# Merged activations kept in SBUF, and dt weight parts stacked, in a hybrid decoder kernel

## Chip, cores and metric

One Trainium2 chip, one of its cores. The metric is the device time of one execution in microseconds, as the median of several.

## What is computed

One layer of a decoder that serves 1024 prompt tokens and 8 x 4 sample tokens, 1056 together, all in fp32. The parts that matter here:

```python
proj = xn @ w_in                      # z | xBC | dt (24 columns) | u | v
dt = softplus(dt_raw + dt_bias)       # 24 heads
a_out = y @ w_a_proj                  # y: (tokens, 1536), after the state space scan
b_out = spatial_gating(u, v) @ w_b_proj
gates = sigmoid(xn @ w_gate + b_gate)
merged = gates[:, :1024] * a_out + gates[:, 1024:] * b_out
x = x + merged @ w_out
x = x + cross_attend(rmsnorm(x), mem_k, mem_v, w_mem_q, w_mem_o)
x = x + hier_moe(x)
```

## The kernel before

Every product is made in three passes (`matmul3`, L277): operands are split into a high part (fp32r) and a low remainder, and high x high, high x low and low x high are accumulated in one PSUM bank. ScalarE makes the high part (a copy), VectorE the low part (a subtraction). The kernel is a row of blocks (stages); the instructions of each engine are written out by hand and tied by semaphores, and all engines meet at a block's end. P is 128, T is 1056, a slab is T / 3 = 352 tokens, BANK is 512 columns, NC = 8 prompt tiles of 128 tokens, NT = 9 with the sample tile, DK = 8 blocks of 128 features.

**stage_rows** (L352) makes v and z by token tiles. After the first round of its nine tiles it makes the dt projection (L541 to L546): for each of three slabs and eight k, one `matmul3` with the 24 weight columns as the stationary operand, so 72 matmuls with 352 moving columns. VectorE copies the result from PSUM to dtT (L744). PE makes the first tile of the next round and then transposes dtT (L531 to L535), and the softplus follows. VectorE makes the low parts of the next weight (L704) ahead of that copy.

**stage_sample_merge** (L1566) ends with eight products, one for each block f of 128 features of merged: 12 k x 3 slabs x 3 passes with the y activations of 1056 columns moving (L1937, a loop on PE). For each f ScalarE and VectorE split the weight (L2017, L2177), VectorE multiplies the gates with the product (`gated`, L2193), GpSimd adds the two gated halves (L1800) into `m_out`, and ScalarE issues the store of that tile to `merged_scr` in HBM (L2056). The last f is gated, added and stored by slabs (L2062, L2208). SyncE loads the gates of the next f once the addition has read them (L1746, L1766). SyncE has loaded the first half of w_out to SBUF in this stage too (`query_w`, L1761). At the end SyncE waits for the stores and reloads the first token tile (L1776), and PE runs eight warming matmuls (`keep_busy`, L1965), each of which is two instructions in the trace.

**stage_out_query** (L2215) starts with `keep_busy` of twelve. Its product is by token tiles: `product(j, c)` for column half j of w_out and tile c, 8 k x 3 passes with 512 columns moving, so 24 matmuls (L2340); `sample_product` is the plain fp32 product of the 32 sample tokens (L2331). The order on PE is product(0,0), sample(0), product(0,1..7), sample(1), product(1,0..7), with the transposes of the normed tiles (`turn`, L2357) from product(1,2) on. Four PSUM banks go round (MB), so a product waits for the addition of the one four places earlier. SyncE (L2272) reloads merged from HBM (sample columns, then three pieces), loads x in one transfer of 4 MB and the sample rows in another, then the second half of w_out in four pieces (each wants its piece of the first half split and two products done), the gain row of the next norm (L2297) and the first four tiles of the query weight (`load_q`). ScalarE (L2403) splits the w_out pieces and the tiles (`w_high`, `high`), VectorE makes the low parts (`w_low`, `low`), and only then adds products to x (`add`, L2493), waiting for all of x (L2519). For the second half it makes w_low(1, 0..3), add(0,7), two query low parts (`q_low`), waits for the gain (L2532), adds the sample product, and then for each tile c: add(1,c), h_low(c-2), normed(c). ScalarE squares each added tile, and GpSimd makes its root mean square (L2318). `turn(c)` waits for normed(c) and h_low(c-1).

## Time and profile before

| | us |
|---|---|
| Median of 3 executions (lowest, highest) | 2085.32 (2078.94, 2086.09) |
| Profiled execution: its time | 2082.61 |
| Its span, first to last instruction | 2080.9 |
| Mean granted TensorE clock, share of full | 0.981 |

The profile is of one execution. Times in it count from the span's start. PE is TensorE's matmuls, PEld its weight loads, DVE VectorE, ACT ScalarE, POOL GpSimd, SP SyncE; an engine's name with a q is its instruction sequencer, which issues DMAs. A matmul's listed duration is longer than the distance to the next, since they are pipelined: for the cost of one, take the distance between starts. "Idle before" is the time in which the engine had nothing running ahead of the instruction, with who released it.

### The profile page before, as it was taken

The page shows a single profiled execution, that of the slowest core. Times are in us where ns is not written, and L with a number is a line of the kernel's source. Part 1 is how long each engine was busy: PE and PEld are TensorE (multiplying, and loading weights), DVE is VectorE, ACT ScalarE, POOL GpSimd, SP SyncE. Part 2 cuts the span into 40 slices and gives each one's busy share as a digit, 9 for nine tenths or more (in the row PEclk, how much of TensorE's full clock was granted, in tenths as well). Part 3 has the DMA queues.
Part 4 walks back from the last instruction along what each step waited for, and adds up shares of the span by engine and source line. Part 5 has one row for each costly group of instructions (what it writes and reads, how often), then busy time and mean ns, then how long its engine had stood idle before and what let it go on. Part 6 is the DMA issues. An engine that isn't in the chain of part 4 may idle for free. (4 is left out here: it accounts for less than half of the span.)

```text
span 2080.9 us, 32851 instructions
## 1 busy us (share of the span) xinstructions
PE 1968.3 (95%) x12220; PEld 1747.1 (84%) x12221; DVE 1033.5 (50%) x1201; ACT 749.7 (36%) x1089; POOL 394.9 (19%) x510
## 2 busy tenths in 40 slices
PE   7999999999999999898999999999999899998995
PEld 5788899999888888788998789888788788877884
DVE  4215254552565656466113341335633675886775
ACT  4322122222334444443002121423412264774674
POOL 2000100000343444431111000000000122223225
PEclk9999999999999999989999999999999899999998
DMA  5122233333334334398546211344404568998987
GB/s 198 58 88 68 67 92 101 82 83 91 97 116 122 111 113 125 103 311 281 180 139 216 84 61 41 107 167 163 154 36 165 205 218 274 331 372 289 318 303 275
DMA packets 247476, 333.02 MB, mean 160 GB/s; under 512 B 16269, under 2 KB 163629, under 8 KB 247329
## 3 DMA queue, kind: packets, MB, share of 16 engines
q1 hardware_dynamic: 211268, 276.25, 39.5%
q0 software_dynamic: 7344, 25.38, 4.7%
q10 hardware_dynamic: 28768, 30.02, 4.1%
q8 instruction: 71, 1.16, 0.2%
q14 instruction: 25, 0.20, 0.0%
HBM read 255.30 MB, written 77.61 MB: 160 GB/s over the span
## 5 line engine op out<-in xcount | busy, mean ns | idle before, releaser
L3932 ACT ACTIVATE e_w_high<-big 128x2048 fp32r<-128x2048 f32 x94 | 176.4, 1911 | 46.4 <-PEq L3018 20.7
L279 PE MATMUL psum<-hT_high,t_w_high 128*128 128x352 f32 x576 | 186.9, 324 | 0.3 <-DVE t_w_low L1022 0.3
L281 PE MATMUL psum<-hT_high,t_w_low 128*128 128x352 f32 x576 | 185.6, 322 | 0.0
L280 PE MATMUL psum<-hT_low,t_w_high 128*128 128x352 f32 x576 | 185.6, 322 | 0.0
L4073 DVE TENSOR_TENSOR e_w_low<-big,e_w_high 128x2048 fp32r<-128x2048 f32 x64 | 144.0, 2288 | 33.1 <-ACT e_w_high L3932 26.2
L279 PE MATMUL psum<-hT_high,s_w_high 128*128 128x352 f32 x384 | 131.8, 343 | 0.0
L280 PE MATMUL psum<-hT_low,s_w_high 128*128 128x352 f32 x384 | 125.1, 326 | 0.0
L281 PE MATMUL psum<-hT_high,s_w_low 128*128 128x352 f32 x384 | 124.8, 325 | 0.0
L3811 PE MATMUL psum<-e_w_high,e_xT 128*128 128x512 f32 x272 | 107.4, 395 | 3.7 <-DVE e_xT L4069 3.0
L279 PEld LDWEIGHTS psum<-hT_high,t_w_high 128*128 128x128 f32 x576 | 108.1, 188 | 0.5 <-DVE t_w_low L1022 0.4
L280 PEld LDWEIGHTS psum<-hT_low,t_w_high 128*128 128x128 f32 x576 | 108.2, 188 | 0.0
L281 PEld LDWEIGHTS psum<-hT_high,t_w_low 128*128 128x128 f32 x576 | 108.1, 188 | 0.0
L3813 PE MATMUL psum<-e_w_high,e_xT 128*128 128x512 f32 x272 | 106.1, 390 | 0.0
L3812 PE MATMUL psum<-e_w_low,e_xT 128*128 128x512 f32 x272 | 106.0, 390 | 0.0
L279 PE MATMUL psum<-r_w_high,hT_high 128*128 128x512 f32 x256 | 101.6, 397 | 4.6 <-DVE hT_low L700 4.6
L280 PE MATMUL psum<-r_w_low,hT_high 128*128 128x512 f32 x256 | 100.5, 392 | 0.0
L281 PE MATMUL psum<-r_w_high,hT_low 128*128 128x512 f32 x256 | 100.4, 392 | 0.0
L4111 DVE TENSOR_TENSOR e_w_low<-big,e_w_high 128x2048 fp32r<-128x2048 f32 x30 | 68.1, 2290 | 52.1 <-ACT e_w_high L3932 52.0
L1040 DVE SCALAR_TENSOR_TENSOR t_conv_out<-t_conv_in,veca,t_conv_out 128x1080 f32<-128x1080 f32 x60 | 80.7, 1344 | 7.5 <-DVE t_conv_out L1040 1.2
L279 PE MATMUL psum<-yT_high,m_w_high 128*128 128x352 f32 x252 | 81.6, 324 | 0.0
L280 PE MATMUL psum<-yT_low,m_w_high 128*128 128x352 f32 x252 | 81.4, 323 | 0.0
L281 PE MATMUL psum<-yT_high,m_w_low 128*128 128x352 f32 x252 | 81.0, 321 | 0.0
(590 smaller groups left out, 4907.0 us busy)
## 6 DMA issues: line engine op xcount, KB each, us to landing
big<-in_w_expert_gate SPq DMA_DIRECT2D x32, 1024.0 KB, 8.3
big<-in_w_expert_up SPq DMA_DIRECT2D x32, 1024.0 KB, 11.0
big<-in_w_expert_down SPq DMA_DIRECT2D x32, 1024.0 KB, 13.3
t_w<-in_w_in SPq DMA_DIRECT2D x24, 512.0 KB, 4.6
m_gates<-gate_scr SPq DMA_DIRECT2D x22, 528.0 KB, 5.7
x_scr<-t_conv_out ACTq DMA_DIRECT2D x20, 512.0 KB, 4.3
gate_scr<-s_gate_tanh ACTq DMA_DIRECT2D x16, 528.0 KB, 3.4
scan_w<-in_w_gate SPq DMA_DIRECT2D x16, 512.0 KB, 4.1
```

What stands on the lines that cost most here:

```text
L279: nc.tensor.matmul(out, ah, w_h, start=start, stop=False)
L280: nc.tensor.matmul(out, ah, w_l, start=False, stop=False)
L281: return nc.tensor.matmul(out, al, w_h, start=False, stop=stop)
L1040: op = nc.vector.scalar_tensor_tensor(o, c[:, j:j + CB_OUT], wk[j], o, ALU.mult, ALU.add)
L3811: nc.tensor.matmul(ps[:, bank, :], ah[:, k, :], w_h, start=(k == 0), stop=False)
L3812: nc.tensor.matmul(ps[:, bank, :], ah[:, k, :], w_l, start=False, stop=False)
L3813: mm = nc.tensor.matmul(ps[:, bank, :], al[:, k, :], w_h, start=False, stop=(k == kt - 1))
L3932: return nc.scalar.activation(dst, src, ACT.Copy)
L4073: nc.vector.tensor_tensor(wl[:, p, :], raw[:, p, :], wh[:, p, :].bitcast(F32), ALU.subtract).then_inc(s_wl, 1)
L4111: nc.vector.tensor_tensor(wl[:, p, :], raw[:, p, :], wh[:, p, :].bitcast(F32), ALU.subtract).then_inc(s_dl, 1)
```

## The change

Three edits.

In stage_rows the high and low parts of the dt weight stand side by side in one tile of 64 columns (24 + 8 zeros, twice). Each k takes two matmuls (high and low activations) instead of three, and the result has the high-weight sums in partitions 0 to 23 and the low-weight sums in 32 to 55. VectorE copies the second to dtT and adds the first. t1 shares its place with wdt.

In stage_sample_merge GpSimd writes each merged tile to its own place in SBUF (five behind `big`, three further up), and nothing is stored to or reloaded from HBM. ScalarE and VectorE split the first 128 tokens of each tile, and after the first half of the last merge product ScalarE makes the four high parts of the first half of w_out; VectorE makes three low parts. PE, in place of the eight warming matmuls, runs k = 0 to 5 of product(0, 0) into PSUM bank 0; k = 6 and 7 follow behind the block's end and the twelve warming matmuls. The loops over f are written out on ScalarE, VectorE and GpSimd.

In stage_out_query x comes in nine transfers, one for each tile with a semaphore of its own, tiles 0, sample, 1 to 5 at once and 6 and 7 once product(0,0) is done. The high and low parts of a token tile are made by two operations each (five tiles of features and three). The gain row, the first query weights, their high parts and the last low piece of the second half of w_out use places of the merged tiles, so they wait for sample(1) (s_mm of order(1, NC) + 1) and for the last low part. The order on the queues: SyncE's gain load goes from before sample(1) to behind it, and `load_q` behind that; ScalarE's `high(0)` stands last of the eight.

```diff
+    HS = 32
...
+        wdt_or_t1 = g.sb("r_wdt_then_t1", [P, NT * H], ctx=ctx)
+        wdt = wdt_or_t1[:, 0:DK * H].rearrange("p (k h) -> p k h", h=H)
+        t1 = wdt_or_t1.rearrange("p (c h) -> p c h", h=H)
+        wdts = g.sb("r_wdt_parts", [P, DK, 2, HS], F32R, ctx=ctx)
+        wdth, wdtl = wdts[:, :, 0, 0:H], wdts[:, :, 1, 0:H]
...
-                            mm = matmul3(nc, ps[0:H, 3 + n, 0:SLAB], wdth[:, k, :], wdtl[:, k, :],
-                                         hh[:, k, xs_], hl[:, k, xs_], k == 0, k == DK - 1)
+                            parts = wdts[:, k].rearrange("p a h -> p (a h)")
+                            nc.tensor.matmul(ps[0:2 * HS, 3 + n, 0:SLAB], parts, hh[:, k, xs_], start=(k == 0), stop=False)
+                            mm = nc.tensor.matmul(ps[0:2 * HS, 3 + n, 0:SLAB], parts, hl[:, k, xs_], start=False,
+                                                  stop=(k == DK - 1))
...
+            nc.vector.memset(wdts[:].bitcast(F32)[:, :, :, H:HS], 0.0)
...
-            nc.vector.tensor_copy(dtT[:, 0:T].rearrange("p (n t) -> p n t", t=SLAB),
-                                  ps[0:H, 3:6, 0:SLAB]).then_inc(s_dte, 1)
+            dt_slabs = dtT[:, 0:T].rearrange("p (n t) -> p n t", t=SLAB)
+            nc.vector.tensor_copy(dt_slabs, ps[HS:HS + H, 3:6, 0:SLAB]).then_inc(s_dtl, 1)
+            dve.wait_ge(s_dtl, 1)
+            nc.vector.tensor_tensor(dt_slabs, dt_slabs, ps[0:H, 3:6, 0:SLAB], ALU.add).then_inc(s_dte, 1)
...
+class OutFirst:
+
+
+    EARLY = 3
     def __init__(self, g):
         alloc = g.nc.alloc_semaphore
-        self.s_stored = [alloc(f"last_merged_stored{n}") for n in range(3)]
-        self.s_first = alloc("first_act_loaded")
-        self.at = g.R1T
-        self.src = g.merged_scr
-
-    def load_first(self, sp):
-
-        sp.wait_ge(self.s_stored[0], 16)
-        sp.dma_start(self.at[:, :, 0:P], self.src[:, :, 0:P].rearrange("k p t -> p k t")).then_inc(self.s_first, 16)
-
-
-def stage_sample_merge(g, top, query_w, act_in):
+        at = g.big_at
+        mix_at = at + 2 * NT * D * 4
+        lower, upper = g.alias32("merged_lower", [P, 5, T], mix_at), g.alias32("merged_upper", [P, 3, T], MERGED_AT)
+        self.parts = ((slice(0, 5), lower), (slice(5, DK), upper))
+        self.tiles = [lower[:, f] for f in range(5)] + [upper[:, f] for f in range(3)]
+        self.ah = g.alias("first_act_high", [P, DK, P], at + (NT + 6) * D * 4)
+        self.al = g.alias("first_act_low", [P, DK, P], at + (NT + 7) * D * 4)
+        piece = [P, 2, BANK]
+        self.wh = [g.alias(f"v_w_high{p}", piece, OUT_PARTS_AT + p * 8192) for p in range(3)]
+        self.wl = [g.alias(f"v_w_low{p}", piece, OUT_PARTS_AT + p * 8192 + 4096) for p in range(3)]
+        self.wh.append(g.alias("v_w_high3", piece, OUT_PARTS_AT - 4096))
+        self.wl.append(g.alias("v_w_low3", piece, OUT_LAST_AT))
+        self.wl_second = self.wl[0:3] + [g.alias("v_w_low3_second", piece, mix_at + 4096)]
+        self.s_wh, self.s_wl, self.s_ah, self.s_al = (alloc("first_out_" + n) for n in (
+            "w_high", "w_low", "act_high", "act_low"))
...
-            sp.wait_ge(s_mst[0], 16 * (DK // 2))
-            sp.wait_ge(s_mst[1], 16 * (DK // 2 - 1))
-
-            sp.wait_ge(s_lm, 3)
-            act_in.load_first(sp)
...
+            for f in range(DK - 1):
+                pool.wait_ge(s_pr, f + 2)
+                nc.gpsimd.tensor_tensor(out.tiles[f], gt[:, 0, :], gt[:, 1, :], ALU.add).then_inc(s_ad, 1)
...
+                nc.gpsimd.tensor_tensor(out.tiles[DK - 1][:, x], gt[:, 0, x], gt[:, 1, x], ALU.add).then_inc(s_la, 1)
...
-            g.keep_busy(6, 8)
+            pe.wait_ge(s_pr, DK)
+            for k in range(2 * out.EARLY):
+                if k % 2 == 0:
+                    pe.wait_ge(out.s_wl, k // 2 + 1)
+                pe.wait_ge(out.s_al, k + 1)
+                matmul3(nc, ps[:, 0, :], out.ah[:, k, :], out.al[:, k, :], out.wh[k // 2][:, k % 2, :],
+                        out.wl[k // 2][:, k % 2, :], k == 0, False)
...
+            def first_high(f):
+                nc.scalar.activation(out.ah[:, f, :], out.tiles[f][:, 0:P], ACT.Copy).then_inc(out.s_ah, 1)
+
+            for f in range(DK - 1):
+                for k in range(2):
+                    if f:
+                        act.wait_ge(s_mh, f * 2 + k + 1)
+                    w_high(f + 1, k, wh)
                 act.wait_ge(s_ad, f + 1)
-                act.dma_start(g.merged_scr[f], mo[:, s, :]).then_inc(s_mst[s], 16)
-
-            tile(0, 0, True, False)
-            with act.Fori(0, DK // 2 - 1) as i:
-                for s in range(2):
-                    tile(i * 2 + 1 + s, 1 - s, True, True)
-            for n in range(3):
-                x = slice(n * SLAB, (n + 1) * SLAB)
-                act.wait_ge(s_la, n + 1)
-                act.dma_start(g.merged_scr[DK - 1][:, x], mo[:, 1, x]).then_inc(act_in.s_stored[n], 16)
+                first_high(f)
+            act.wait_ge(s_qw, 64)
+            act.wait_ge(s_mh, 2 * DK - 1)
+            for p in range(out.EARLY + 1):
+                nc.scalar.activation(out.wh[p][:], query_raw[:, 2 * p:2 * p + 2, :], ACT.Copy).then_inc(out.s_wh, 1)
+            act.wait_ge(s_la, 1)
+            first_high(DK - 1)
...
+            def first_low(f):
+                dve.wait_ge(out.s_ah, f + 1)
+                tt(out.al[:, f, :], out.tiles[f][:, 0:P], out.ah[:, f, :].bitcast(F32), ALU.subtract).then_inc(out.s_al, 1)
+
+            def out_w_low(p):
+                dve.wait_ge(out.s_wh, p + 1)
+                tt(out.wl[p][:], query_raw[:, 2 * p:2 * p + 2, :], out.wh[p][:].bitcast(F32), ALU.subtract).then_inc(out.s_wl, 1)
+
+            for f in range(DK - 1):
+                following(f)
+                gated(f, 3 * (f % 2))
+                if f:
+                    first_low(f - 1)
+            first_low(DK - 2)
+            out_w_low(0)
+            out_w_low(1)
             dve.wait_ge(s_gt, DK * 32)
             for n in range(3):
+                if n == 1:
+                    out_w_low(2)
                 x = slice(n * SLAB, (n + 1) * SLAB)
                 dve.wait_ge(s_lm, n + 1)
                 stt(gt[:, 0, x], gt[:, 0, x], 1.0, ps[:, 3 + n, 0:SLAB], ALU.add, ALU.mult).then_inc(s_lg, 1)
-
-
-def stage_out_query(g, x, x_dram, w, qT, qT_at, kv_at, mem, act_in):
+            first_low(DK - 1)
...
+            def load_x(t):
+                src = d["x_prompt"][0][t * P:(t + 1) * P, :] if t < NC else d["x_sample"].rearrange("b t n -> (b t) n")
+                sp.dma_start(x[0:rows(t), t, :], src).then_inc(s_x[t], 16)
+
+            load_x(0)
+            sp.wait_ge(s_z, 1)
+            load_x(NC)
+            for t in range(1, 6):
+                load_x(t)
+            sp.wait_ge(s_mm, 1)
+            for t in range(6, NC):
+                load_x(t)
             for p in range(PW):
                 sp.wait_ge(s_wl, p + 1)
                 sp.wait_ge(s_mm, 2)
                 load_w(1, p)
+            sp.wait_ge(s_mm, order(1, NC) + 1)
+            sp.wait_ge(s_al, NC)
...
+                first = j == 0 and c == 0
+                if j == 0 and c:
+
+                    pe.wait_ge(s_al, c)
+                if j and c == 0:
+                    pe.wait_ge(s_al, NC)
                 if n >= MB:
                     pe.wait_ge(s_ad, n - MB + 1)
-                for k in range(DK):
+                for k in range(2 * out.EARLY if first else 0, DK):
                     if c == 0 and k % 2 == 0:
                         pe.wait_ge(s_wl, PW * j + k // 2 + 1)
-                    mm = matmul3(nc, ps[:, n % MB, :], ah[:, k, cols(c)], al[:, k, cols(c)], wh[:, k, :],
-                                 wl[:, k, :], k == 0, k == DK - 1)
+                    a_h, a_l = (out.ah[:, k, :], out.al[:, k, :]) if first else (ah[:, k, cols(c)], al[:, k, cols(c)])
+                    mm = matmul3(nc, ps[:, n % MB, :], a_h, a_l, wh[k // 2][:, k % 2, :],
+                                 wls[j][k // 2][:, k % 2, :], k == 0, k == DK - 1)
...
+            act.sem_inc(s_wh, PW)
...
+                for k, part in out.parts:
+                    op = nc.scalar.activation(ah[:, k, cols(c)], part[:, :, cols(c)], ACT.Copy)
+                op.then_inc(s_ah, 1)
...
-            w_high(0, 0)
-            high(0)
-            for p in range(1, PW):
-                w_high(0, p)
             for c in range(1, NC):
                 high(c)
+            high(0)
             for p in range(PW):
                 w_high(1, p)
+            act.wait_ge(s_mm, order(1, NC) + 1)
+            act.wait_ge(s_al, NC)
             for q in range(2):
                 q_high(0, q)
...
+            dve.sem_inc(s_wl, out.EARLY)
...
+                dve.wait_ge(s_ah, c if c else NC)
+                for k, part in out.parts:
+                    op = nc.vector.tensor_tensor(al[:, k, cols(c)], part[:, :, cols(c)], ah[:, k, cols(c)].bitcast(F32),
+                                                 ALU.subtract)
+                op.then_inc(s_al, 1)
...
+                    dve.wait_ge(s_x[c], 16)
...
+            w_low(0, PW - 1)
             for c in range(1, NC):
                 low(c)
-            dve.wait_ge(s_x, 16 * len(x_dram))
+            low(0)
             add(0, 0)
             add_sample(0, order(0, NC))
             for c in range(1, NC - 1):
                 add(0, c)
-            for p in range(PW):
+            for p in range(PW - 1):
                 w_low(1, p)
             add(0, NC - 1)
+            dve.wait_ge(s_mm, order(1, NC) + 1)
+            w_low(1, PW - 1)
             dve.wait_ge(s_wl, 2 * PW)
-            dve.wait_ge(s_mm, order(1, NC) + 1)
             for q in range(2):
                 q_low(q, q)
             dve.wait_ge(s_gr, 16)
```

## Rows read from the trace of the kernel before

**Rows 1.** The page, part 1: busy time of each engine.

```profile
...
PE 1968.3 (95%) x12220; PEld 1747.1 (84%) x12221; DVE 1033.5 (50%) x1201; ACT 749.7 (36%) x1089; POOL 394.9 (19%) x510
```

**Rows 2.** Waits, 1100 to 1240 us: who waited, for whom, total, times, longest.

```profile
...
DVE big L2497 <- DMA big<-in_x_sample: 8.7, 1, 8.7
...
PE psum L279 <- DVE big L2497: 4.6, 1, 4.6
...
PE psum L128 <- PEq L133: 2.0, 1, 2.0
PE psum L2362 <- DVE R_low L2506: 1.8, 2, 0.9
```

**Rows 3.** Groups by line, 60 to 95 us: count, busy and mean ns, idle before.

```profile
...
L279 PEld LDWEIGHTS psum<-hT_high,r_wdt_high 128*24 128x24 f32 x24 | 2.4, 101 | 1.5 <-issue 0.2
...
L744 DVE COPY r_dtT<-psum 24x1056 f32<-24x1056 f32 x1 | 1.2, 1245 | 11.1 <-PE psum L281 11.1
```

**Rows 4.** Timeline of PE, dt projection: start, length, operation.

```profile
...
73.55 0.34 PE L279 MATMUL psum<-hT_high,r_wdt_high 128*24 128x352 f32 x1
...
85.04 0.39 PE L279 MATMUL psum<-r_w_high,hT_high 128*128 128x512 f32 x1
...
90.59 0.73 PE L533 MATMUL psum<-ident,r_dtT 24*128 24x24 f32 x9
```

**Rows 5.** Groups by line, 1070 to 1112 us, in the merge.

```profile
...
L279 PEld LDWEIGHTS psum<-yT_high,m_w_high 128*128 128x128 f32 x87 | 16.3, 188 | 0.0
...
L2179 DVE SCALAR_TENSOR_TENSOR m_w_low<-m_w,m_w_high 128x768 fp32r<-128x768 f32 x4 | 3.8, 958 | 28.4 <-ACT m_w_high L2019 28.4
```

**Rows 6.** Timeline of PE, from the last merge product to the second half.

```profile
...
1115.08 1.95 PE L128 MATMUL psum<-ident 128*128 128x128 f32 x16
1119.07 4.54 PE L128 MATMUL psum<-ident 128*128 128x128 f32 x24 [2.05 <-PEq L133]
1123.37 0.48 PE L279 MATMUL psum<-v_w_high,v_act_high 128*128 128x512 f32 x1
...
1129.02 1.95 PE L2336 MATMUL psum<-v_w,big 128*32 128x128 f32 x64
...
1141.69 0.39 PE L281 MATMUL psum<-v_w_high,R_low 128*128 128x512 f32 x1
1146.68 0.47 PE L279 MATMUL psum<-v_w_high,v_act_high 128*128 128x512 f32 x1 [4.61 <-DVE big L2497]
...
1175.70 1.95 PE L2336 MATMUL psum<-v_w,big 128*32 128x128 f32 x64
1177.58 0.50 PE L279 MATMUL psum<-v_w_high,v_act_high 128*128 128x512 f32 x1
```

**Rows 7.** Busy time by window: length, each engine's busy (count), PEclk, DMA share.

```profile
...
1147.00:1151.00 4.00, 4.00 (x12) 3.14 (x11) 1.87 (x5) 0.00 (x0) 0.00 (x0) 0.57 1.05 380
```

**Rows 8.** Timeline of ACT, end of the merge stage.

```profile
...
1112.03 5.14 ACTq L2065 DMA_DIRECT2D merged_scr<-m_out  x3
```

**Rows 9.** Timeline of DVE after the second sample product.

```profile
...
1178.70 2.35 DVE L2511 TENSOR_TENSOR v_q_w_low<-v_q_w,v_q_w_high 128x1024 fp32r<-128x1024 f32 x2
...
1183.35 0.69 DVE L2497 TENSOR_TENSOR big<-big,psum 128x512 f32<-128x512 f32 x1 [1.22 <-PE psum L281]
...
1188.79 0.69 DVE L2497 TENSOR_TENSOR big<-big,psum 128x512 f32<-128x512 f32 x1 [1.33 <-PE psum L281]
...
1197.27 1.23 DVE L2506 TENSOR_TENSOR R_low<-psum,v_act_high 128x1024 fp32r<-128x1024 f32 x1 [2.34 <-ACT v_act_high L2434]
```

**Rows 10.** Timeline of PE, the second transpose of the output stage.

```profile
...
1200.37 1.03 PE L2362 MATMUL psum<-ident,v_xn 128*128 128x128 f32 x8
```

**Rows 11.** DMA issues, whole run: destination, queue, KB each, us to landing.

```profile
...
big<-in_x_prompt SPq DMA_DIRECT2D x1, 4096.0 KB, 20.5
...
gain_row<-in_norm_mix SPq DMA_DIRECT2D x1, 512.0 KB, 5.2
```

**Rows 12.** The same, 1178 to 1240 us.

```profile
...
v_q_w<-in_w_mem_q SPq DMA_DIRECT2D x2, 512.0 KB, 4.5
```

More of the change, by code:

```diff
@@ L138 @@
 OUT_W_AT = 212960
+MERGED_AT = 197952
+OUT_PARTS_AT = 120032
+OUT_LAST_AT = 181472
 SUMS_AT = 221696
@@ L429, in _ @@
             with nc.allow_non_contiguous_dma(reason="24 columns of dt"):
[L430 removed]
+                sp.dma_start(wdt, w_in[:, :, COL_DT:COL_DT + H]).then_inc(s_wdt, 16)
             sp.dma_start(w[:, 1], w_in[:, :, first_col[1]:first_col[1] + BANK]).then_inc(s_w[1], 16)
@@ L633, in _ @@
             act.wait_ge(s_wdt, 16)
-            nc.scalar.activation(wdth[:], wdt[:], ACT.Copy).then_inc(s_dh, 1)
+            nc.scalar.activation(wdth, wdt, ACT.Copy).then_inc(s_dh, 1)
             act.wait_ge(first.s_alog, 16)
@@ L721, in _ @@
             dve.wait_ge(s_dh, 1)
-            nc.vector.tensor_tensor(wdtl[:], wdt[:], wdth[:].bitcast(F32), ALU.subtract).then_inc(s_dl, 1)
+            nc.vector.tensor_tensor(wdtl, wdt, wdth.bitcast(F32), ALU.subtract).then_inc(s_dl, 1)
             for c in range(2, NT):
@@ L753, in _ @@
             ch.done(nc.vector.tensor_scalar(g.dt[:], t2[:], 0.0, None, ALU.max))
-            ch.done(nc.vector.tensor_tensor(g.dt[:], g.dt[:], t1[:], ALU.add))
+            ch.done(nc.vector.tensor_tensor(g.dt[:], g.dt[:], t1, ALU.add))
             ch.done(nc.vector.tensor_tensor(g.dta[:], g.dt[:], mid(g.aneg[:], NT), ALU.mult))
@@ L763, in _ @@
             dve.wait_ge(s_act, 4)
-            ch.done(nc.vector.tensor_tensor(g.dte[:], g.dt[:], t1[:], ALU.mult))
+            ch.done(nc.vector.tensor_tensor(g.dte[:], g.dt[:], t1, ALU.mult))
             w_low(3)
@@ L1657, in stage_sample_merge @@
         s_mh, s_pr, s_ad = g.sem("m_half_product"), g.sem("m_gated"), g.sem("m_added")
-        s_mst = [g.sem(f"m_stored{i}") for i in range(2)]
         s_lm, s_lg, s_la = (g.sem("m_last_" + x) for x in ("product", "gated", "added"))
@@ L2046, in _ @@
             act.wait_ge(s_bm, CHUNKS)
-            def tile(f, s, more, waits):
-                if more:
-                    for k in range(2):
-                        if waits:
-                            act.wait_ge(s_mh, f * 2 + k + 1)
-                        w_high(f + 1, k, wh)
-                act.wait_ge(s_ad, f + 1)
-                act.dma_start(g.merged_scr[f], mo[:, s, :]).then_inc(s_mst[s], 16)
-            tile(0, 0, True, False)
-            with act.Fori(0, DK // 2 - 1) as i:
-                for s in range(2):
-                    tile(i * 2 + 1 + s, 1 - s, True, True)
-            for n in range(3):
-                x = slice(n * SLAB, (n + 1) * SLAB)
-                act.wait_ge(s_la, n + 1)
-                act.dma_start(g.merged_scr[DK - 1][:, x], mo[:, 1, x]).then_inc(act_in.s_stored[n], 16)
+            def first_high(f):
[5 more added lines that the diff above has]
+                    w_high(f + 1, k, wh)
+                act.wait_ge(s_ad, f + 1)
+                first_high(f)
[5 more added lines that the diff above has]
+            first_high(DK - 1)
         @block.vector
@@ L2238, in stage_out_query @@
         s_w = [[g.sem(f"v_w_loaded{j}_{p}") for p in range(PW)] for j in range(2)]
-        s_x, s_gr = g.sem("v_x_loaded"), g.sem("v_gain_loaded")
-        s_a = [g.sem(f"v_act_loaded{i}") for i in range(AP_)]
-        s_as = g.sem("v_sample_act_loaded")
+        s_x, s_gr = [g.sem(f"v_x_loaded{t}") for t in range(NT)], g.sem("v_gain_loaded")
         s_uw = [g.sem(f"v_q_w_loaded{i}") for i in range(2)]
-        s_z, s_az, s_mm, s_ad, s_ah, s_al, s_wh, s_wl, s_wf = (g.sem("v_" + n) for n in (
-            "x_padded", "act_padded", "product", "added", "act_high", "act_low", "w_high", "w_low", "w_parts_used"))
+        s_z, s_mm, s_ad, s_ah, s_al, s_wh, s_wl, s_wf = (g.sem("v_" + n) for n in (
+            "x_padded", "product", "added", "act_high", "act_low", "w_high", "w_low", "w_parts_used"))
         s_sq, s_ms, s_rs, s_xn, s_tr, s_hh, s_hl = (g.sem("v_" + n) for n in (
@@ L2316, in _ @@
             nc.gpsimd.memset(x[:, NT - 1, :], 0.0).then_inc(s_z, 1)
-            nc.gpsimd.memset(act_T[:, :, T:TP], 0.0).then_inc(s_az, 1)
             for c in range(NT):
@@ L2511, in q_low @@
                 nc.vector.tensor_tensor(ul[:, q], uw[:, q], uh[:, q].bitcast(F32), ALU.subtract).then_inc(s_ul, 1)
-            w_low(0, 0)
-            low(0)
-            for p in range(1, PW):
-                w_low(0, p)
+            w_low(0, PW - 1)
             for c in range(1, NC):
                 low(c)
-            dve.wait_ge(s_x, 16 * len(x_dram))
+            low(0)
             add(0, 0)
```

92 lines of the change are left out of this document (20 added, 72 removed).

## The prediction

> **What bounds the kernel now.** I first read the busy shares of the page: PE works 95% of the span, no other engine over half [rows 1]. So a change pays where it takes matmuls off PE, or removes a hole in PE's stream. Next I read the waits of the stretch that the diff touches [rows 2]. PE has three holes there: 2.0 us at the stage boundary, 4.6 us waiting for an addition on VectorE, and 1.8 us in two late transposes. VectorE itself sat 8.7 us behind the load of x, so the second hole is x arriving late. The timeline puts it between the third and the fourth output product [rows 6]. After it the granted clock is 0.57 of full for four microseconds, so for most of them the lower level, 1.2 GHz [rows 7]. Last, the dt projection: 72 matmuls without a hole from 73.55 to 85.04 us, 0.1596 us each [rows 4].
>
> **The dt projection.** It goes from 72 matmuls to 48: high and low columns of the weight stand together as 64 weight columns, and each is multiplied by high and low activations. 24 x 0.1596 = 3.83 us less on PE. What no row shows is a weight load of 64 columns. One of 24 takes 101 ns [rows 3] and one of 128 takes 188 [rows 5]; but beside the 128-column loads, too, 264 matmuls of 352 columns pass in 42 us (three groups like that of the row), 0.159 each. So the load is hidden at both sizes and I take 0. Were it not hidden, interpolation gives 34 ns more for each of 48, 1.6 us back. The Trainium skill (TensorE: Matmul & The Clock Gate, "Back-to-back issue gap" and "LDWEIGHTS") says that the spacing is set by both operations and that a load takes columns / 1.2 ns; by that, as an estimate, 53 ns against 20, and the saving would be 2.2 us instead of 3.8. The equal spacings at 24 and at 128 columns speak against it.
>
> The parts must now be added on VectorE: after the copy of 1.25 us comes an addition of about the same length. It is hidden. VectorE had waited 11.1 us for this product [rows 3], and PE wants dtT only behind one more product, 5.55 us later [rows 4]; 2 x 1.25 plus a semaphore leaves 2.8 us. The memset of the padding columns and the strided writes of the parts fall into VectorE's and ScalarE's idle time at the start; t1 taking wdt's place moves nothing.
>
> **Across the stage boundary.** The eight warming matmuls (16 instructions, 1.95 us) go [rows 6]. In their place come 18 matmuls of the first output product (k 0 to 5), about 0.23 us each, so 4.1 us of work that was behind the boundary: moved, not saved. The last arrival there was PE at 1117.03 and ScalarE, issuing stores, at 1117.17 [rows 6, 8]. Now PE arrives alone at 1115.08 + 18 x 0.23 + 0.16 of drain = 1119.4, and I keep the 2.04 us of boundary and the twelve warmers with their 4.3 us behind it. Saved: 1.95 - 0.16 = 1.79. An accumulation left open in PSUM over a boundary stands in no row; it waits for nothing, so 0, and at worst one more boundary, 2.0.
>
> Its cover: the operands must be ready by 1115. The output weight's four high parts start when the first half of the last merge product is through, 54 x 0.16 = 8.6 before 1115.08, so at 1106.4; four ScalarE copies of about 1.05 end at 1110.7. VectorE makes two low parts (1.2 each, from 128x768 at 0.96 [rows 5]) before the last gates, the third after the first gate slab; it is there by about 1114 and wanted 12 matmuls after 1115. The 128x128 splits of each merged tile (two per tile, each under 0.3) and the unrolled loops of the three engines lie in merge products of 108 x 0.16 = 17.3 us. The merged stores and reloads (4.3 MB each way) vanish and no one on the path waits for their absence except as follows.
>
> **x per tile.** x used to queue behind the merged reload, landing 20.5 us after its issue [rows 11]. Now x tile 0 is the first transfer of the new stage. At about 400 GB/s a 512 KB tile is 1.3 us; five tiles and the sample are there some 9 us after the boundary, the last two, which wait for the first product, by 12. VectorE adds tile 0 only after its nine splits. These are now pairs of operations because the merged tiles lie in two places. A pair is between 1.2 (one of 128x1024) and 1.9 (two of 0.96 [rows 5]); I take 1.4, near the sum of elements plus one start. 1.2 + 8 x 1.4 = 12.4, the first addition ends at 13.1 after the boundary; the fourth product wants it at 4.3 + 1.5 + 2.0 + 10.9 = 18.7. With 1.9 it is 17.1, still in time. So the hole goes: from 1141.92 to 1146.68, 4.76 us, and with it 4.0 x (1 - 0.57) = 1.72 us of slow clock [rows 6, 7]. Next late is nothing until the second half.
>
> **What is moved back.** The gain row and the first two query weights used to be issued around 1140 us. Now they alias the merged tiles and wait for the second sample product (call its end T, 1177.58 before [rows 6]). ScalarE's and VectorE's query splits wait with them, and VectorE's additions stand queued behind. The price: a gain broadcast landed 5.2 us after its issue [rows 11]; two more 512 KB transfers behind it at 1.3 each: the second query weight lands at T + 0.1 + 5.2 + 2.6 = T + 7.9. The bounds are 4.7, a query pair alone [rows 12], with nothing for the gain, and 20.5, the worst load there is [rows 11]. After landing, its high and low part end 2.26 later, T + 10.2; before, that was 1181.05, T + 3.5 [rows 9]: 6.7 late. Slack: VectorE's idle 1.22, 1.33 and again 1.33 before three additions [rows 9], then 1.87 between the first low part done at 1198.50 and the transpose that wants it at 1200.37 [rows 9, 10]. Together 5.8, so PE loses 0.9 us: the landing less 7.0. From then on VectorE catches up 1 us per tile.
>
> **The sum** against the profiled execution (2082.61 us, span 2080.9): -3.83 - 1.79 - 4.76 - 1.72 + 0.9 = -11.2, giving 2071.4. The median shown is 2.7 above that execution, so 2085.3 - 11.2 = 2074.1. A measurement of this kernel can tell about 0.5%, 10.4 us, from no change; the forecast is barely over it.
>
> **Rivals.**
> (a) The moved loads bite harder. If they land as crowded as the old stage's loads, say 13 us after issue, the loss is 13.4 - 7.0 = 6.4 plus 1.7 of clock behind the new hole: 12.1 - 8.1 = 4.0 left, 2081. For: these loads are now on a wait chain. Against: nothing else uses the queue at that moment, and a pair took 4.5 [rows 12]. Chance 0.12.
> (b) The same place, on the other side: a landing of 20.5 [rows 11] costs 13.5 + 1.7 = 15.2 against 12.1, so +3.1, 2088.4. It decides from a landing of 17.4. That needs eight times the megabytes in the queue. Chance 0.03.
> (c) The x hole only changes its name: additions late behind VectorE's splits or a tile of x. Then the 6.5 us stay, 2080.6. It needs 5.6 us of extra delay. Chance 0.07.
> (d) Part of the change does not do what it says: the 64-column weight loads show (1.6 back) or the boundary takes longer (up to 2.0). 2076 to 2078. Chance 0.12.
> The forecast itself: 0.66.
>
> **How the numbers follow.** The best case has no loss at T and reads 2073.2 against the median; the three executions shown spread over 7 us, which I allow as 3.5 either way, and the median stood near their upper end, so low 2067.5. Upwards (d) and most of (a) and (c) are taken in: 2080.5. Faster by over 0.5% needs under 2074.9: of the forecast's 0.66 about 0.48, of (d) 0.03, and 0.03 for a low draw of the rest, 0.54. Slower by over 0.5% needs +10.4, far over (b)'s price, so it takes an unforeseen cause: 0.04. The rest, 0.42, is within.
>
> **What would show it.** 48 matmuls of 352 columns in the dt projection at 0.16 apart, dtT read without a hole; 18 matmuls between the last merge product and the boundary and no warmers; the output stage's first half from boundary to second sample product 48 us instead of 58.5, with no VectorE wait on x and a clock of 1.00; the second query weight landing near T + 8 and about 1 us of new PE wait before the second or third transpose. Wrong would be a weight-load-bound dt spacing, a hole over 2 us after T, or PE waiting at 1115 for the output weight's low parts.

## The result and the profile after

The changed kernel takes 2066.16 us (median; 2063.97 to 2067.87 over 4 runs), the kernel before 2082.94 beside it (2078.94 to 2086.09): ratio 0.9917, interval 0.9904 to 0.9929, so 16.8 us less by the medians where 11.2 were forecast, and 1.3 under the forecast's lower end of 2067.5. The profiled executions differ by 16.7 (2082.61 and 2065.92; spans 2080.9 and 2064.0). The forecast of 2074.1 also stood on a median of three, 2085.3, which is 2.4 above the later one; the other 5.6 us are gain that it did not see.

TensorE's busy time fell from that of [rows 1] by 14.3 us; the other engines do slightly more. The page of the changed kernel, part 1:

```profile
PE 1954.0 (95%) x12180; PEld 1737.1 (84%) x12181; DVE 1036.8 (50%) x1219; ACT 753.2 (36%) x1105; POOL 399.3 (19%) x509
```

**The dt projection**, groups by line (60 to 95 us), then the timeline of PE, against [rows 3, 4]:

```profile
L550 PE MATMUL psum<-hT_high,r_wdt_parts 128*64 128x352 f32 x24 | 7.7, 324 | 0.0
...
L551 PEld LDWEIGHTS psum<-hT_low,r_wdt_parts 128*64 128x64 f32 x24 | 3.2, 135 | 0.6
```

```profile
73.78 0.37 PE L550 MATMUL psum<-hT_high,r_wdt_parts 128*64 128x352 f32 x1
...
81.52 0.39 PE L282 MATMUL psum<-r_w_high,hT_high 128*128 128x512 f32 x1
```

48 matmuls in 7.74 us are 0.161 each: the 64-column loads take 135 ns, between the 101 and 188 that bounded them, and do not show in the spacing.

**From the merge to the output stage**, timeline of PE, against [rows 6]:

```profile
1108.81 0.39 PE L282 MATMUL psum<-v_w_high,first_act_high 128*128 128x512 f32 x1
...
1112.69 0.39 PE L284 MATMUL psum<-v_w_high,first_act_low 128*128 128x512 f32 x1
1114.80 2.92 PE L128 MATMUL psum<-ident 128*128 128x128 f32 x24 [1.73 <-PEq L133]
1117.47 0.48 PE L282 MATMUL psum<-v_w_high,first_act_high 128*128 128x512 f32 x1
```

The 18 moved matmuls run without a gap. But the boundary's idle time is 1.73 us, not 2.05, and the same 24 warming instructions take 2.92 us, not 4.54: the granted clock over them and their wait is 1.00 of full, where it was 0.60 in the kernel before, the lower of its two levels for most of the time. From the first of them to the end of the second sample product it is 46.3 us, where the prediction wrote 48. There is no hole for x; from here on PE has no wait longer than a microsecond to the second sample product, which ends at 1161.12. **Behind it** ScalarE, then PE's transpose:

```profile
1167.53 1.06 ACT L2448 ACTIVATE v_q_w_high<-v_q_w 128x1024 fp32r<-128x1024 f32 x1 [7.07 <-DMA v_q_w<-in_w_mem_q]
1169.12 1.06 ACT L2448 ACTIVATE v_q_w_high<-v_q_w 128x1024 fp32r<-128x1024 f32 x1 [0.53 <-DMA v_q_w<-in_w_mem_q]
```

```profile
1184.77 1.06 PE L2374 MATMUL psum<-ident,v_xn 128*128 128x128 f32 x8 [0.70 <-DVE R_low L2522]
```

The second query weight is there 8.0 us behind the end of the sample product (forecast 7.9), and PE loses 0.9.

Read by PE's milestones (the starts of the first matmuls of each part), the change of each stretch, in us, in two pairs of profiles (the second pair, taken later, is e11 and e12):

| stretch | forecast | first pair | second pair |
|---|---|---|---|
| start of the run to the dt projection | 0 | +0.2 | +1.4 |
| dt projection | -3.8 | -3.75 | -3.75 |
| from there to the first product of the next stage | 0 | -0.9 | -0.8 |
| to the first merge product | 0 | -1.9 | -1.0 |
| merge, boundary, first half of the output stage | -8.3 | -10.2 | -10.0 |
| second half, to the first query product | +0.9 | +0.9 | +1.0 |
| all that follows | 0 | -0.8 | -1.6 |
| to the last matmul | -11.2 | -16.4 | -14.7 |

So the forecast terms came as forecast, and three things came on top: 1.9 us at the boundary, 0.8 to 0.9 behind the rows stage, and 2.6 to 2.7 spread over other stages, against which 0.2 and 1.4 were lost ahead of the dt projection.

### The profile page after: what moved, and what is told of

It is laid out like the page before. It is cut to its first block and busy times, and to the rows that moved or that the text cites. A ratio compares the mean times of both kernels' runs of the same rounds, so it can differ in the third digit from the quotient of the medians.

```text
span 2064.0 us, 32742 instructions
## 1 busy us (share of the span) xinstructions
PE 1954.0 (95%) x12180; PEld 1737.1 (84%) x12181; DVE 1036.8 (50%) x1219; ACT 753.2 (36%) x1105; POOL 399.3 (19%) x509
```

## The experiments

All times of the kernel before beside them lie at 2082.3 to 2083.6 (medians of 7 to 19 executions), but for e16's single 2084.2. A gain is taken from the ratio. Where there is one execution (e9, e10, e11, e13, e14, e16), its time means little and the trace decides.

**The parts alone.** e1 is the kernel before with only the dt edit; e2 is the changed kernel with the dt edit undone.

> The kernel before with the dt edit alone. Both theories: the dt projection 3.8 us shorter on PE (24 matmuls of 352 columns at 0.16), nothing of it given back. Theory A (chance: the part of the gain beyond the sum of terms is granted clock that happened to fall at stage boundaries in the profiled execution of before and not in that of after): -3.5 to -3.8 us in time, and the profile shows slow stretches at some of the boundaries near 521, 1115 and 1491 us, in no fixed pattern. Theory B (the boundaries behave by what runs around them): the 3.5 us earlier arrival changes nothing at the boundaries, slow stretches near 1115 as in the profile of before.

> The changed kernel with the dt projection as it was. By the terms of the prediction without dt: 1.8 (warmers) + 4.8 (wait for x) + 1.7 (clock behind it) - 0.7 (the moved loads, as the profile of after shows it) = -7.6 us. Theory A: -7.6 on average, with a spread of 2 us by the clock. Theory B (the first output products ahead of the boundary keep the clock up over it): -9.6 to -10, and the twelve warmers take 2.7 us in the profile, not 4.3.

e1: 2078.18, ratio 0.9979 (0.997 to 0.9988), 4.4 us less; its milestones are at -3.4 behind the dt projection, -4.3 at the next stage's start. e2: 2072.83, ratio 0.9954 (0.994 to 0.9967), 9.6 less. In e2's profile the stretch from the merge to the second sample product is shorter by 10.2 us, as in the changed kernel; that profile is of the fastest of its five executions (2066.99), 5.8 below their median. The sum of the two is 14.0 with an uncertainty of 3.4; nothing shows that the parts work on each other. The dt edit makes 0.9 us at a place that it doesn't touch (below).

**The first output product back behind the boundary (e3)**, with its eight warmers ahead:

```diff
-            pe.wait_ge(s_pr, DK)
-            for k in range(2 * out.EARLY):
-                ...
+            g.keep_busy(6, 8)
...
-                for k in range(2 * out.EARLY if first else 0, DK):
+                for k in range(DK):
```

> The changed kernel, but with all 24 matmuls of product(0,0) behind the boundary and the eight warming matmuls ahead of it again. By the sum it gives back 1.8 us of the gain against before (ratio from about 0.9917 to 0.9926). Theory A: that and no more on average; the warmers behind the boundary take 2.7 or 4.3 us as the clock happens to be. Theory B: 1.8 + 1.6 = 3.4 us given back (ratio about 0.9933), and the warmers take 4.3 us.

2068.33, ratio 0.9932 (0.9919 to 0.9946). From the merge's end to the second sample product it stands 1.7 us behind the changed kernel, the 1.79 forecast for the warmers. Yet its boundary has 1.72 us of idle time and a full clock, so e2's theory B, that the first products ahead of the boundary keep it up, is out:

```profile
1113.02 2.92 PE L128 MATMUL psum<-ident 128*128 128x128 f32 x24 [1.72 <-PEq L133]
```

**x in tiles alone (e4):** the kernel before, its stores and reloads kept, with x in nine transfers with a semaphore each.

```diff
+            for t in range(NC):
+                sp.dma_start(x[:, t, :], d["x_prompt"][0][t * P:(t + 1) * P, :]).then_inc(s_xt[t], 16)
+                if t == 0:
                     sp.wait_ge(s_z, 1)
-                sp.dma_start(dst, src).then_inc(s_x, 16)
+                    sp.dma_start(x_dram[1][0], x_dram[1][1]).then_inc(s_xt[NC], 16)
...
+                if j == 0:
+                    dve.wait_ge(s_xt[c], 16)
...
-            dve.wait_ge(s_x, 16 * len(x_dram))
```

> The kernel before with x in nine transfers, one semaphore for each tile, still behind the reload of merged. The hole of 4.6 us before the fourth output product should go, and with it 1.7 us of slow clock: -6.5 us, since VectorE's first addition then waits for its own splits (done at 1137) and not for all 4 MB. Rival: the transfers share the engines, so tile 0 lands late all the same behind 4 MB of merged; then it is less than -3 and a wait on x stays in the profile.

2076.83, ratio 0.9971 (0.9961 to 0.9981): 6.0 less. By the milestones the merge, the boundary and the first half are 6.5 shorter. The waits of the stretch name no VectorE wait on x and no PE wait on an addition; only the late transposes' 1.8 us and the boundary remain:

```profile
PE psum L128 <- PEq L133: 2.1, 1, 2.1
```

**x in two transfers (e15):** the changed kernel with six tiles, then two.

```diff
-            load_x(0)
+            load_many(0, 6)
             sp.wait_ge(s_z, 1)
             load_x(NC)
-            for t in range(1, 6):
-                load_x(t)
             sp.wait_ge(s_mm, 1)
-            for t in range(6, NC):
-                load_x(t)
+            load_many(6, NC)
```

> The changed kernel with x for the output stage in two transfers (six tiles, then two) in place of eight, the sample's by itself as before. Theory A (with the merged result's reload gone, x is early enough however it is cut): the six tiles, 3 MB, land by some 12 us behind the boundary, TensorE has no hole, the shift at the second sample product is as in the changed kernel, 2066.5. Rival (x per tile is needed too): VectorE's first addition waits for the whole of it, so TensorE waits for a free bank, 1 to 3 us more, or the clock falls behind it.

2066.39, ratio 0.992 (0.9904 to 0.9937); merge end to second sample product -10.1 against before, as in the changed kernel (-10.2). So the tiles by themselves remove the hole (e4), and with the reload gone two transfers are as good as nine (e15). Their gains don't add, and cutting x finer than in two earns nothing once the reload is gone. That the reload's absence is enough with x in one transfer of 4 MB was not run.

**Who brings the clock down at the boundary.** Before, e1 and e4 (stores and reload there) had 2.05 us idle and a slow clock; the changed kernel, e2 and e3 had 1.7 and a full one. In the former ScalarE arrived last, with its stores [rows 8]. e6 and e9 are e3 with one copy on ScalarE behind GpSimd's last addition, of 128 and of 384 columns, and no stores (shown is e9's):

```diff
             first_high(DK - 1)
+            act.wait_ge(s_la, 3)
+            nc.scalar.activation(ps[:, 0:3, SLAB:SLAB + P],
+                                 out.tiles[DK - 1][:, T - 3 * P:T].rearrange("p (b n) -> p b n", n=P), ACT.Copy)
```

> The variant with all of the first output product behind the stage boundary, and one more copy of 128x128 on ScalarE at the end of the merge block, which waits for GpSimd's last add, so that ScalarE is the last engine to arrive, some 0.35 us after it, as it was in the kernel before with its stores; there are no stores. Theory A (the boundary's idle time and the clock behind it hang on who arrives last, not on the stores' traffic): TensorE idle 2.0 to 2.1 us instead of 1.72, clock at its lower level behind it, twelve warmers and the wait to 4.3 us, in all 1.9 us more than without the copy, so about 2070.2. Theory B (it is the stores' and the reload's traffic or chance): idle 1.7, warmers 2.7 us, clock full, no difference from 2068.3.

> The variant of the late copy with three times the columns (128x384), so that ScalarE ends some 0.55 us behind GpSimd's last add (the copy of 128x128 ended 0.31 behind it, TensorE then stood idle 1.82 us at the boundary and the clock stayed full). Theory A (a longer idle time at this boundary is what brings the clock down, whoever makes it, no stores needed): idle 2.05 to 2.1 us, the lower clock behind it, twelve warmers and the wait 4.3 us instead of 2.7. Theory B (the stores, the reload or chance bring it down): idle 2.05 to 2.1, clock full, 2.7 us.

Timelines of ACT and PE, e6 first:

```profile
1112.14 0.28 ACT L2065 ACTIVATE psum<-merged_upper 128x128 f32<-128x128 f32 x1 [3.99 <-POOL merged_upper L1810]
```

```profile
1114.14 2.92 PE L128 MATMUL psum<-ident 128*128 128x128 f32 x24 [1.82 <-PEq L133]
```

```profile
1112.93 0.49 ACT L2065 ACTIVATE psum<-merged_upper 128x384 f32<-128x384 f32 x1 [3.99 <-POOL merged_upper L1810]
```

```profile
1115.15 4.54 PE L128 MATMUL psum<-ident 128*128 128x128 f32 x24 [2.03 <-PEq L133]
```

e6 missed its own mark: the copy delayed the boundary by 0.1 us only, PE idled 1.82 and the clock stayed full (median 2066.6 of four, from 2065.04 to 2071.08, the last being the profiled one). With 2.03 us (e9, a single 2071.92) the clock falls, to 0.60 of full over the warmers and their wait, and these take their 4.54 us, without a store or a reload; from the merge's end to the second sample product e9 is 1.95 us longer than e3. Of the 18 profiles of this study, eight had 1.72 to 1.82 us there and the clock stayed full in all; ten had 2.03 to 2.05 and it fell in nine (it held in e14). So a last arrival 0.3 us later cost 0.3 + 1.6 = 1.9 us here, and that is the size of what the vanished stores gave. e9 is one profile, and e14 shows that the longer idle time does not always bring the fall.

**The end of the rows stage.** All kernels with the dt edit as it stands idled 0.67 us there, the unedited ones 1.4 to 1.7, behind four last stores on ScalarE that nobody edited. e5 shifts those stores' tile by 96 bytes (the edit's shift beyond a multiple of 512), e10 is the edit with 24 matmuls of 352 columns more:

```diff
+        g.sb("r_z_offset", [P, 24], ctx=ctx)
         zs = g.sb("r_z", [P, 3, BANK], ctx=ctx)
```

```diff
+                    for k in range(3 * DK):
+                        nc.tensor.matmul(ps[:, 7, 0:SLAB], hh[:, k % DK, 0:P], hl[:, k % DK, 0:SLAB], start=True, stop=True)
                     for n in range(3):
```

> The kernel before, with 96 bytes left free ahead of the tile r_z in the rows stage and nothing else. In the three profiled kernels that hold the dt edit the wait for the last projection stores is shorter by 1.0 us (TensorE idle 0.67 us at the end of the rows stage where the others have 1.44 to 1.74) and the last four stores of r_z are issued in 1.75 us where the others take 2.5 to 2.8. No instruction there is changed by the dt edit, but its other tiles move r_z by 608 bytes, which is 96 beyond a multiple of 512. Theory A (the place of r_z sets how long these stores take): issue 1.75 us, idle 0.67, some 1.0 us less than the kernel before, about 2081.5. Theory B (the place has nothing to do with it; it is the shorter dt chain or chance): issue 2.5 to 2.8, idle 1.4 to 1.7, no difference.

> The dt edit alone, with 24 matmuls of 128x128 by 352 columns more ahead of the 48, into a bank that nobody reads, so that TensorE runs as many matmuls for as long as in the kernel before, while tiles, places and VectorE's parts are those of the edit. The six profiled kernels with the edit issue the last four r_z stores in 1.75 us and have 0.67 us idle behind them, the five without it 2.5 to 2.8 and 1.4 to 1.7. Theory A (what differs is the layout of the tiles or the two operations of VectorE): 1.75 us and 0.67 us stay, 3.8 us longer than the dt edit alone. Theory B (it is when the stage runs, or how many matmuls its program has): 2.5 to 2.8 us and 1.4 to 1.7 us, as before.

e5: 2082.07, ratio 0.9998 (0.9989 to 1.0007), stores in 2.48 us, idle 1.39. The place is not it. e10 (a single 2083.41): 2.43 and 1.34, so the edit's layout and VectorE's part are not it either; what was restored is the number of matmuls and their time. The transfers of a queue that the profile calls one of instructions then gave a candidate: where the stores take long, one of 16 KB lies among them. Before, DMA from 225.3 to 229.6 us (kind: packets, MB, share), then ACT and PE:

```profile
q8 instruction: 1, 0.02, 1.7%
```

```profile
225.34 2.65 ACTq L653 DMA_DIRECT2D z_scr<-r_z  x4
```

```profile
229.63 2.47 PE L128 MATMUL psum<-ident 128*128 128x128 f32 x20 [1.57 <-PEq L362]
```

After, the same view from 221.8 to 225.1 us has no row of that kind; the transfer comes at 227.35.

```profile
221.81 1.76 ACTq L660 DMA_DIRECT2D z_scr<-r_z  x4
```

Three kernels move it by 16-column matmuls ahead of the dt product: 24 on the edit alone (e13), 24 and 96 on the kernel before (e14, e16; the loop runs over 12 * DK there).

```diff
+                    for k in range(3 * DK):
+                        nc.tensor.matmul(ps[:, 7, 0:16], hh[:, k % DK, 0:P], hl[:, k % DK, 0:16], start=True, stop=True)
```

> The dt edit alone, with 24 matmuls of 16 columns more ahead of its 48: the program has as many matmuls as before, while the stage ends at most some 1 to 2 us later than with the edit alone. The 14 traces so far show a transfer of 16 KB on an instruction queue (q8): in those with the long program (five, and e10) it stands at 225.5 to 226.5 us, among the last four r_z stores, which take 2.4 to 2.8 us to issue; in those with 24 matmuls fewer it stands at 226.6 to 228.4, behind the boundary, and the stores take 1.75 us. Theory A (a fetch of instructions that comes due at that count of instructions collides with the stores): the fetch is among the stores again, 2.4 to 2.8 us and 1.3 to 1.75 us idle, so the 1.0 us is lost though the time of the stage hardly changes. Theory B (it is the moment, not the count): 1.75 and 0.67.

> The kernel before with 24 matmuls of 16 columns more ahead of its 72. Theory A (fetch by count of instructions): the fetch comes due 24 instructions sooner, some 5 us ahead of the last stores, so these issue in 1.75 us and TensorE's idle time at the end of the rows stage is 0.67 instead of 1.44 to 1.57: added work of about 1 us buys back 1.0 there. Theory B: 2.5 and 1.5, and the kernel is 1 us slower.

> The kernel before with 96 matmuls of 16 columns more in the rows stage (24 of them moved the fetch too little: what precedes it in the program are 64 narrow matmuls of 0.03 us each, so it still stood at 227.33 among the stores from 227.72 on). 96 instructions back from the fetch are some 5 of the warmers, the 64 narrow ones and 27 of the last wide product at 0.227 us, so it comes due 8 us ahead of the last stores. Theory A (it comes due by count and slows the stores beside it): no 16 KB transfer of q8 between the first of the last four stores and the boundary, the stores issue in 1.75 us, TensorE idles 0.67 us there instead of 1.34 to 1.74, while the kernel is 10 to 11 us slower for the added matmuls. Theory B (the fetch has nothing to do with it): 2.4 to 2.8 and 1.3 to 1.7 again.

e13 (2084.21): transfer at 226.92, stores 2.64 us, idle 1.55. That agrees with its theory A, but the short matmuls took 2.94 us and the clock fell beside them, so time was restored too and the rival is not excluded. e14 (2088.05) gave what its theory B said, 2.56 and 1.47 us. But the transfer had hardly moved: it runs from 227.24 to 228.96, across the first of the stores, which are issued from 227.72 on. So e14 decides nothing. What I had mis-worked is the transfer's path: the 24 instructions ahead of it are of the 64 narrow ones of 0.03 us. e16 goes past those. It is a single 2100.01, 15.9 slower than the kernel before where 10 to 11 were expected, since its 96 short matmuls ran mostly at the low clock. The transfer stands at 237.3, nine microseconds ahead of the stores, and, in the kernel before's own code for this stage's end:

```profile
246.41 1.76 ACTq L655 DMA_DIRECT2D z_scr<-r_z  x4
```

```profile
249.81 2.47 PE L128 MATMUL psum<-ident 128*128 128x128 f32 x20 [0.67 <-PEq L362]
```

In the 18 profiles the stores took 1.75 us wherever no such transfer lay among them, and 2.4 to 2.8 wherever one did. That such a transfer beside the stores costs 0.7 to 1.1 us of idle time here is borne out by all 18 and by e16, which moved it away; why it slows their issue is not shown, nor whether the count of instructions alone sets when it comes.

**Is the rest chance?** Second profiles of both kernels, and five more executions of the changed one:

> The kernel before, a second profile. Asked is which of its falls of the clock are its own and which are chance. The falls at the merge boundary (1120), behind the x hole (1147) and in the sample stage (866 to 972) are expected again; the ones at the scan's start (526, 2.7 us) and in the attention stage (1495, 1.1 us) stood in three of the four profiled kernels without the change's dt part and in one of six with it. Theory A (chance): either may be missing here. Theory B (the kernel's own): both are there.

> The changed kernel, a second profile and five more rounds, for a closer mean. Expected: 2066.1, no fall at the merge boundary, 0.67 us idle at the end of the rows stage. Theory A (the clock at the scan's start is chance): it falls there in this profile or in some of its runs, and the time spreads over 3 us or more. Theory B: it never falls there, and no run is above 2067.9.

e11: 2080.85. e12: 2067.01 (2065.49 to 2068.92), ratio 0.993 (0.9917 to 0.9942). Boundary and rows stage repeat in both. e11 gave its theory B, both falls. e12 gave neither theory whole: the clock did not fall at the scan's start in its profile, but two of its times lie above 2067.9.

At the scan's start the clock fell in both profiles of before (worth 2.8 to 3.1 us over the next 100 matmuls), in neither of the changed kernel; but with the same idle time there (1.41 to 1.45 and 1.03 to 1.04 us in all), it fell in e8, e9 and e15, which have the changed kernel's rows stage, and not in e2, which has the one of before, nor in e16. So this fall is not tied to an edit; that it comes less often in the faster kernels (3 of 9 profiles with the dt edit as it stands, 7 of 9 of the rest) remains a tendency, not explained.

Behind the attention stage it is otherwise. All nine profiles without the output edit have 1.77 to 1.83 us of idle time at that boundary, all nine with it 1.34, and the clock fell at it in seven of the former (not in e1 and e16) and in one of the latter (e12). Timelines of PE: e14, with the fall, and e15, without:

```profile
1501.37 4.99 PE L128 MATMUL psum<-ident 128*128 128x128 f32 x28 [1.77 <-PEq L133]
1481.19 3.36 PE L128 MATMUL psum<-ident 128*128 128x128 f32 x28 [1.34 <-PEq L133]
```

The shorter idle time gives nothing by itself: from its start to the next product there are 5.4 us in either group where the clock stays up (5.2 in e2). With the fall there are 6.0 to 6.5 (7.7 in e5), so what goes with the output edit here is some 1 us of clock. That the shorter idle time is the reason is not shown: in e5 and e11 the clock had fallen some 2 us before that idle time began. No instruction of this stage is changed, and what shortens the idle time stays open.

**Two further versions.** In e7 the gain row is issued behind the first two query weights, and VectorE waits for it only at the first tile that it scales. e8 adds to that the sample's output product in the place of the twelve warmers:

```diff
-            sp.dma_start(gr[:], g.flat["norm_mem"].partition_broadcast(P)).then_inc(s_gr, 16)
...
             load_q(0)
+            sp.dma_start(gr[:], g.flat["norm_mem"].partition_broadcast(P)).then_inc(s_gr, 16)
```

```diff
-            g.keep_busy(TB, 12)
+            sample_product(0, order(0, NC))
             product(0, 0)
-            sample_product(0, order(0, NC))
```

> The changed kernel with the load of the gain row issued behind the first two query weight loads on SyncE, and VectorE's wait for it moved to the first tile that it scales. Forecast: the second query weight lands at 3 us instead of 8.0 behind the end of the second sample product, VectorE's lows of the query weights stand before the memory of the rows is wanted and the 0.9 us between the second sample product and the first query product (-16.46 to -15.54 in the shift against before) come back: 2065.2. Rival: the row then lands later than it is wanted and costs the same or more: no difference, or up to 1 us slower.

> e7, and the sample's first output product (its own loads are there by then) stands in the place of the twelve warming matmuls behind the boundary, ahead of the last two thirds of the first output product. Forecast: the 2.67 us of warmers and wait go, as the sample's product fills the time until VectorE has the last parts: 2.7 us less than e7, 2062.5. Rival: the sample's product, narrow matmuls right behind an idle boundary, starts at the lower clock and lasts longer, or waits for its weights' load, so the gain is under 1.5 us.

e7: 2066.02, ratio 0.9914 (0.99 to 0.9928). The loss behind the second sample product is gone, 0.0 instead of 0.9 by the milestones, though the second query weight is there only at T + 6.1, not at 3. By its time e7 cannot be told from the changed kernel (2066.16 and 2067.01). e8: 2062.53 (2059.41 to 2063.91), ratio 0.9901 (0.9886 to 0.9915). PE's timeline at the boundary:

```profile
1117.24 1.30 PE L2344 MATMUL psum<-v_w,merged_lower 128*32 128x128 f32 x40 [1.73 <-PEq L133]
1118.33 0.87 PE L2344 MATMUL psum<-v_w,merged_upper 128*32 128x128 f32 x24
1119.13 0.50 PE L282 MATMUL psum<-v_w_high,first_act_high 128*128 128x512 f32 x1
```

The sample's product now stands in the warmers' place and runs at the full clock: merge end to second sample product is 2.9 us shorter than in e7 (forecast 2.7). e8 has the lowest median of the study, though the intervals of its ratio and of e7's overlap; that the 2.9 us are its own is read from the trace.

## Why the prediction was wrong

**The dt projection:** right. 3.75 us against 3.83; the load of 64 columns is hidden. The Trainium skill (TensorE: Matmul & The Clock Gate, "Back-to-back issue gap") says that the spacing is set by both operations; the estimate made from it, 2.2 saved, does not hold here: the spacing stayed 0.161 beside a load of 135 ns, and the measurement decides. VectorE's added operation cost PE nothing.

**Across the boundary:** the warmers' removal gave its size (1.7 by e3 against 1.79). The step that failed is "I keep the 2.04 us of boundary and the twelve warmers with their 4.3 us behind it". I had noted ScalarE's stores as the last arrival, saw that PE would arrive alone without them, and still left the boundary's length and the clock behind it as they were. In truth the boundary shrinks to 1.73, and with that the clock stays up: -0.3 and -1.6 (e3 against e9). I had priced the slow clock behind the x hole, from the window's 0.57 [rows 7], and overlooked that the 4.3 us for twelve warmers was the same sign: 24 instructions in 4.54 us there, 16 in 1.95 just before it [rows 6].

**x:** hole and its slow clock went as forecast, 6.5 against e4's 6.5 by milestones. The reason was told too narrowly: I gave tiles and reload together, and the tiles do it alone (e4), as does the reload's absence with x in two transfers (e15). Of the rivals, (c) fell with that.

**Moved loads:** the landing at 8.0 for 7.9 and the loss 0.9 for 0.9. e2, e3 and e6 show 2.2 to 2.7 with a landing of 9.3 to 9.8, so the term has a spread of 1.8 us, by the prediction's own rule, the landing less 7.0. None comes near the 6.4 of rival (a). That the forecast's 0.9 was met so closely in the changed kernel is luck in part.

**Not in the sum at all:** 0.9 us at the end of the rows stage (e5, e10, e16), since with 24 matmuls fewer a transfer of the instruction queue no longer lies among the last stores; and 2.6 us in other stages, mostly falls of the clock. The one at the scan's start looks like chance; the one behind the attention stage, some 1 us, goes with the output edit. The prediction put all these at nothing without giving a reason; no instruction at these places is edited. And the base, the median of three, was 2.4 us high; I had seen that it stood near its upper end and allowed for it in the range, not in the forecast. The range, 2067.5 at its lower end, was drawn only for that spread, with no term for gains that the sum doesn't hold. Such terms were looked for on the side of losses alone.

## What to carry to other kernels

When an edit takes an engine's last work before a stage boundary away, ask what the boundary's idle time becomes and in which state the clock comes out: a group of warmers that is longer per instruction behind a gap than ahead of it says that the clock fell there, and that 0.3 us of earlier arrival can be worth 1.9. If two parts of a change remove the same wait, price it once and try each alone. Put real, ready work where warmers stand (e8). And read the boundaries that no edit touches too: two of them gave 0.9 and some 1 us here.

## What was not expected of the hardware

- At one boundary the clock stayed full behind 1.82 us of idle time and fell behind 2.03, with the same work around it (e6, e9). The bound is not sharp: in e14 it held behind 2.05, and at another boundary it fell beside 1.77 (before, e10, e13, e14).
- Beside one 16 KB transfer of an instruction queue, 0.9 to 1.7 us long, four small stores were issued on ScalarE in 2.4 to 2.8 us instead of 1.75 and landed in 1.8 to 2.1 us instead of 1.5. Adding or removing matmuls 150 us earlier decided whether they met (e10, e16).
- Matmuls of 16 columns with 128-column weights pass at 0.12 us each at full clock (24 in 2.85, e14) and at 0.19 with the low one beside them (96 in 18.57, e16), so they were no cheap filler here.
- GpSimd's addition of 128x352, 0.95 us otherwise, took 1.86 beside a VectorE subtraction of 128x1024 in the changed kernel; it was not on the path.
